# PEER block: U's two halves are summed on VectorE in place of TensorE, and semaphores stand in place of the drains in VectorE's chunk

## What is computed

```python
def chunk(args):
    ht, it, gt = args
    u = eu[it]
    a = jax.nn.gelu(jnp.einsum('ckd,cd->ck', u, ht).astype(jnp.float32), approximate=False) * gt
    return jnp.einsum('ck,ckd->cd', a.astype(ht.dtype), ev[it])
```

## Time and profile before

| | us |
|---|---|
| median of 3 runs | 1521.03 (1520.96 to 1522.51) |
| the profiled execution | 1529.37 |
| its span, first to last instruction | 1527.6 |
| PE busy in the span | 1489.6 (98%) |
| DVE busy | 1333.8 (87%) |
| POOL busy | 1028.9 (67%) |
| ACT busy | 760.4 (50%) |

### The profile page before, as it was taken

The page is one execution under the profiler, slowest core; times in us unless marked ns, Lnnn a source line. Parts: engine busy times, 40 slices in busy tenths (PEclk is TensorE's granted clock), DMA queues, the critical chain, the costliest instruction groups (busy, mean ns, idle before and its releaser), DMA issues.

```text
span 1527.6 us, 21852 instructions
## 1 busy us (share of the span) xinstructions
PE 1489.6 (98%) x7296; PEld 1236.3 (81%) x7296; DVE 1333.8 (87%) x2237; ACT 760.4 (50%) x1179; POOL 1028.9 (67%) x732
## 2 busy tenths in 40 slices
PE   7999999999999999999999999999999999999998
PEld 5887778888887888888878888888887888788886
DVE  6497666688998999989969999999999999999997
ACT  4644442433455555555455555454544555455553
POOL 6643224333886777778877777777777777777771
PEclk8999999899999999999999999999999999999999
DMA  9335447222776998989889999999999999999993
GB/s 361 98 104 173 154 149 266 79 83 83 220 237 191 284 293 278 293 278 315 285 299 396 396 389 401 370 377 393 393 388 360 380 398 395 368 390 395 396 404 129
DMA packets 219582, 444.58 MB, mean 291 GB/s; under 512 B 22360, under 2 KB 128984, under 8 KB 219232
## 3 DMA queue, kind: packets, MB, share of 16 engines
q1 hardware_dynamic: 174432, 309.04, 57.5%
q0 software_dynamic: 45056, 134.38, 23.1%
HBM read 407.68 MB, written 35.67 MB: 290 GB/s over the span
## 4 chain that ended last, share of the span: by engine, by line
PE 56%; POOL 27%; issue 8%; DMA 4%; DVE 3%; ACT 1%; DVEq 0%; SPq 0%; ACTq 0%; POOLq 0%
POOL coef L684 14%; POOL rows L678 13%; PE ps L1756 8%; PE ps L1757 8%; PE ps L1758 8%; PE ps L1505 4%; PE ps L1507 4%; PE ps L1506 4%; PE ps L1836 4%; PE ps L1805 2%; PE ps L1808 2%; PE ps L1811 2%; PE ps L1770 2%; PE ps L1838 2%; DMA coef<-gelu_spill,coef_at 2%
## 5 line engine op out<-in xcount | busy, mean ns | idle before, releaser
L635 POOL TENSOR_TENSOR wlo<-raw,whi 128x1024 fp32r<-128x1024 f32 x178 | 428.8, 2422 | 294.3 <-ACT whi L714 293.9
L1836 PE MATMUL ps<-acts,whi 128*128 128x512 f32 x1024 | 366.3, 397 | 0.0
L684 POOL DMA_INDIRECT coef<-gelu_spill,coef_at x256 | 299.5, 1170 | 82.0 <-issue 77.8
L678 POOL DMA_INDIRECT rows<-w_stream,row_at x256 | 273.0, 1067 | 78.0 <-issue 76.5
L1838 PE MATMUL ps<-acts,wlo 128*128 128x256 f32 x1024 | 287.3, 281 | 0.0
L714 ACT ACTIVATE whi<-raw 128x1024 fp32r<-128x1024 f32 x176 | 186.2, 1060 | 150.1 <-PE ps L1758 104.5
L1836 PEld LDWEIGHTS ps<-acts,whi 128*128 128x128 f32 x1024 | 192.7, 188 | 46.3
L1756 PE MATMUL ps<-whi,acts 128*128 128x512 f32 x512 | 200.7, 392 | 2.8 <-DVE gate_lo L1336 2.1
L1757 PE MATMUL ps<-wlo,acts 128*128 128x512 f32 x512 | 200.3, 391 | 0.0
L1758 PE MATMUL ps<-whi,acts 128*128 128x512 f32 x512 | 199.8, 390 | 0.0
L1838 PEld LDWEIGHTS ps<-acts,wlo 128*128 128x128 f32 x1024 | 193.6, 189 | 5.2
(11 more groups left out here) (253 smaller groups left out, 2582.8 us busy)
## 6 DMA issues: line engine op xcount, KB each, us to landing
raw<-w_stream SPq DMA_DIRECT2D x304, 512.0 KB, 5.4
values_in<-w_stream SPq DMA_DIRECT2D x128, 512.0 KB, 7.6
ada<-w_ada SPq DMA_DIRECT2D x32, 512.0 KB, 4.7
gelu_spill<-gout SPq DMA_DIRECT2D x64, 256.0 KB, 5.4
gate_spill<-gblock SPq DMA_DIRECT2D x8, 2048.0 KB, 10.4
gates<-gate_spill SPq DMA_DIRECT2D x32, 512.0 KB, 8.3
ada<-w_ada SPq DMA_DIRECT2D x32, 256.0 KB, 7.2
rows<-w_stream,row_at POOLq DMA_INDIRECT x256, 7.1
```

The source lines that it names most:

```text
L635: g.tensor_tensor(wlo[:, s, :], raw[:, s, :], whi[:, s, :].bitcast(F32), ALU.subtract)\
L678: g.indirect_dma_start(rows[m % ROWS][:, :], None, w_front.rearrange("c p n -> (c p) n"), bass.IndirectOffsetOnAxis(row_at[:, t * P + n:t ...
L684: g.indirect_dma_start(coef[:, t, n:n + 1], None, gelu_dram.rearrange("t p g (e o) -> (t p g e) o", o=1), bass.IndirectOffsetOnAxis(coef_a ...
L1836: mm(ps[:, 6 + e % PAIRED, :].rearrange("p (n t) -> p n t", n=2), wh, acts[:, :, k, 0:HALF], start=k == 0, stop=False)
```

## The change

`add_low` and its identity matrix go. VectorE gets `add_again(e)`, which adds `u_again(e, 0)` and `ulow` into a new SBUF tile `usum`; GELU reads `usum`. `again(e + 2)` on TensorE waits for that sum (it overwrites the bank) instead of for the GELU. The drains of the chunk go; `add_row(n, 0)` waits on semaphores instead, and `scale_coefs` is done at the end of the chunk before the one that needs it. GpSimd issues the coefficients of `n + 1` ahead of the rows of `n`.

```diff
@@ -221,8 +221,8 @@
         gelus = [gout[:, 2 * t:2 * t + 2, :].rearrange("p s n -> p (s n)") for t in range(PAIR)]
         prod = at("prod", 4, [P, RING, HALF], F32)
 
-        ulow = at("ulow", 24, [P, 2, HALF], F32R)
-        ident_r = at("ident_r", 26, [P, P], F32R)
+        usum = at("usum", 24, [P, 2, HALF], F32)
+        ulow = at("ulow", 26, [P, 2, HALF], F32)
         value_hi, value_lo = (w[:, PAIRED:2 * PAIRED, :] for w in (whi, wlo))
         phi = at("phi", 18, [P, PAIRED, HALF], F32R)
         plo = at("plo", 20, [P, PAIRED, HALF], F32R)
@@ -697,9 +697,9 @@
             for n in range(FIRST_COEFS):
                 fetch_coefs(n)
             for n in range(FIRST_ROWS, NK):
-                fetch_rows(n)
                 if n + FIRST_COEFS - FIRST_ROWS < NK:
                     fetch_coefs(n + FIRST_COEFS - FIRST_ROWS)
+                fetch_rows(n)
 
 
         @block.scalar
@@ -941,8 +941,6 @@
                 act.wait_ge(prod_ready, e + 1)
                 a.activation(phi[:, s % PAIRED, :], prod[:, s % PAIRED, :], ACT.Copy).then_inc(phi_ready, 1)
 
-            a.activation(ident_r[:, :], ident[:, :], ACT.Copy).then_inc(ident_ready, 1)
-
             def v_step(e, q, s, chunk=True, take=True):
 
                 act.wait_ge(chunk_used, e + (C_E + 1))
@@ -954,7 +952,7 @@
                     act.wait_ge(prod_ready, e - (RING - 1))
                 if PAIRED <= e < PAIRED + RING:
                     act.wait_ge(gelu_stored[s // 2], 16 * (NK // RING + 1))
-                a.activation(gelu_of(e), u_again(e, 0), ACT.Gelu).then_inc(gelu_done, 1)
+                a.activation(gelu_of(e), usum[:, e % 2, :], ACT.Gelu).then_inc(gelu_done, 1)
                 prod_hi(e, s)
                 if take:
                     value_take(e + 1, q + (s + 1) // RING, (s + 1) % RING)
@@ -1421,16 +1419,15 @@
             def scale_coefs(b):
                 dve.wait_ge(coef_in[b % COEF_RING], 16 * PAIR * COEFS * (b // COEF_RING + 1))
                 some = slice(b * COEFS, (b + 1) * COEFS)
-                v.tensor_tensor(coef[:, :, some], coef[:, :, some], gate_of[:, :, some], ALU.mult)
-                dve.drain()
+                v.tensor_tensor(coef[:, :, some], coef[:, :, some], gate_of[:, :, some], ALU.mult).then_inc(coefs_scaled, 1)
 
             def add_row(n, t):
 
+                m = n * PAIR + t
                 if t == 0:
-                    dve.drain()
-                    if n % COEFS == 0:
-                        scale_coefs(n // COEFS)
-                m = n * PAIR + t
+                    if n >= 1:
+                        dve.wait_ge(row_added, m)
+                    dve.wait_ge(coefs_scaled, n // COEFS + 1)
                 dve.wait_ge(row_in[m % ROWS], 16 * (m // ROWS + 1))
                 row, factor = rows[m % ROWS][:, :], coef[:, t, n:n + 1]
                 total = acc[:, t, :] if n == NK - 1 else sums[t]
@@ -1453,12 +1450,20 @@
                 v.tensor_tensor(plo[:, e % PAIRED, :], prod[:, e % PAIRED, :], phi[:, e % PAIRED, :].bitcast(F32),
                                 ALU.subtract).then_inc(plo_ready, 1)
 
+            def add_again(e):
+                dve.wait_ge(u_low_taken, e + 1)
+                v.tensor_tensor(usum[:, e % 2, :], u_again(e, 0), ulow[:, e % 2, :], ALU.add).then_inc(u_added, 1)
+
             make_value_lo(0)
             weights_normed(1)
             dve.drain()
             v.tensor_copy(gate_of[:, :, :].rearrange("p t n -> p (t n)"), fetched[2])
+            dve.drain()
             for e in range(NK):
                 due = [(n, t) for n in range(rows_done(e), rows_done(e + 1)) for t in range(PAIR)]
+                if e == BEHIND:
+                    scale_coefs(0)
+                add_again(e)
                 for n, t in due[:1]:
                     add_row(n, t)
                 make_prod(e)
@@ -1467,6 +1472,9 @@
                 prod_lo(e)
                 for n, t in due[1:]:
                     add_row(n, t)
+                for n in range(max(1, rows_done(e + 1)), rows_done(e + 2)):
+                    if n % COEFS == 0:
+                        scale_coefs(n // COEFS)
                 if e + 1 < NK:
                     make_value_lo(e + 1)
 
@@ -1811,22 +1819,18 @@
                     last = mm(dense_sums(t, half), plo[:, slot, column(t)], vh, start=False, stop=final, skip_group_check=True)
                 return last
 
-            def add_low(e):
-                pe.wait_ge(u_low_taken, e + 1)
-                mm(u_again(e, 0), ident_r[:, :], ulow[:, e % 2, :], start=False, stop=True,
-                   skip_group_check=True).then_inc(u_added, 1)
-
             def v_tile(e, s, final=False):
                 last = split_products(e, 1, final)
                 if final:
                     last.then_inc(dense_done, 1)
+                split_products(e, 0, final).then_inc(dense_done if final else values_used, 1)
+
+            def again(e, s):
+
+                if e >= PAIRED:
+                    pe.wait_ge(u_added, e - PAIRED + 1)
                 else:
-                    add_low(e + 1)
-                split_products(e, 0, final).then_inc(dense_done if final else values_used, 1)
-
-            def again(e, s):
-
-                pe.wait_ge(gelu_done, NK + 1 + e)
+                    pe.wait_ge(gelu_done, NK + 1 + e)
                 if not isinstance(e, int) or e >= POOL_LO:
                     pe.wait_ge(u_lo_ready, e - (POOL_LO - 1))
                 else:
@@ -1844,8 +1848,6 @@
                 mm(ps[:, b, 0:1], ident[:, :], zero[:, :], start=True, stop=True)
             for e in range(PAIRED):
                 again(e, e)
-            pe.wait_ge(ident_ready, 1)
-            add_low(0)
             for e in range(NK - PAIRED):
                 v_tile(e, e)
                 again(e + PAIRED, e)
@@ -1861,7 +1863,7 @@
                 turn(pair)
             v_tile(NK - 2, NK - 2)
             for n, pair in enumerate(TURNED_ORDER[2:]):
-                pe.wait_ge(gelu_done, 2 * NK + 1 + n)
+                pe.wait_ge(u_added, NK - 1 + n)
                 turn(pair)
             v_tile(NK - 1, NK - 1, final=True)
 
```

More of the change, by code:

```diff
@@ L365, in build @@
         u_low_taken = sem("u_low_taken")
-        ident_ready = sem("ident_ready")
         u_first_done = sem("u_first_done")
@@ L389, in build @@
         row_added = sem("row_added")
+        coefs_scaled = sem("coefs_scaled")
         turned = sem("turned")
@@ L1822, in v_tile @@
                     last.then_inc(dense_done, 1)
-                else:
-                    add_low(e + 1)
                 split_products(e, 0, final).then_inc(dense_done if final else values_used, 1)
             def again(e, s):
-                pe.wait_ge(gelu_done, NK + 1 + e)
+                if e >= PAIRED:
+                    pe.wait_ge(u_added, e - PAIRED + 1)
+                else:
+                    pe.wait_ge(gelu_done, NK + 1 + e)
                 if not isinstance(e, int) or e >= POOL_LO:
```

## The result

The changed kernel takes 1580.86 us (median of 4 runs, 1576.23 to 1583.62), the kernel before 1521.77 on the same chip: a ratio of 1.0373 [1.0333, 1.0413]. The forecast was 1525, with a range of 1516 to 1535. The direction was right, the size was not. The profiled execution took 1583.62 us, its span is 1581.8.

A forecast was written before the change was run, and what follows sets the result against it. It took VectorE's issue time plus its waits to be the V stage, with TensorE and GpSimd full too. Chunk work +9.3, waits -4.5 and the end -1 gave +3.8 us on 1521.0: 1525, range 1516 to 1535.

The forecast's parts named there:

- TensorE off the path: V stage: TensorE loses the identity product, 0.12 us a chunk, but VectorE needs more, so worth nothing by itself.
- The sum costs 0.33: VectorE's chunk: the added 256-column sum takes 0.33 us to the next start, at most 0.42.
- The rival with the sum not overlapped: VectorE's chunk: the sum costs 0.42 us in place of 0.33, +11 us, 1536; chance 0.13.
- the larger price for PSUM: VectorE's sum: by the skill's fixed cycles it would cost 0.065 us more, an estimated 8 us over the run.
- The drain and the scaling: VectorE's chunk: a drain less saves 0.17 us, and scaling falls from 0.24 to 0.07.
- parts 1 to 3 and 5: V stage: TensorE's relief nothing, VectorE's sum less drains and scaling +9.3 us, the end of the run -1 us.
- Four a chunk again: V stage: GpSimd still fits four fetches a chunk; VectorE's waits fall from 14.8 to 10.3 us, -4.5 us.
- Over 20 us of waits: Sign of a wrong forecast: VectorE's waits over 20 us; 6 to 14 us in all would be right.
- The end: Last chunks: the sum needn't wait behind TensorE's work, but VectorE, GELU and prod stand in a row: -1 us (0 to -2).
- GpSimd out of step: V stage: a fetch slips behind one more held instruction, 1.5 us; twelve slips are +18 us, 1540; chance 0.09.
- C: Theory of the experiments, V stage: the new fetch order makes rows late.

The follow-up runs named there:

- e9: Changed kernel without the second token group's coefficient fetches, so three fetches per pick: 1521.99 us, ratio 0.9993.
- e14: Kernel before without the second token group's coefficient fetches, three per pick: 1514.07 us, where the kernel before takes 1644.7.
- e7: Kernel before with only the fetch order swapped, coefficients ahead of rows: 1524.23 us, ratio 1.0011.
- e12: Kernel before with identity product kept on TensorE, no chunk drains, scaling a chunk ahead, coefficients fetched first: 1590.71 us, ratio 1.0426.
- e8: Changed kernel with one drain at the chunk's end, ahead of value_lo: 1549.03 us, ratio 1.0173.
- e11: Changed kernel with one drain ahead of each pick's first row: 1561.34 us, ratio 1.0252.
- e18: Changed kernel with one drain between plo and the second row: 1547.81 us, ratio 1.0157.
- e3: Kernel before with only the sum moved to VectorE, with old drains, scaling and order: 1577.97 us, ratio 0.9652, on a slow chip.
- e1: Changed kernel with one drain ahead of each pick's first row, on a slow chip: 1578.55 us, ratio 0.9659.
- e2: Changed kernel with rows fetched ahead of coefficients again, on a slow chip: 1614.9 us, ratio 0.988.
- e13: Changed kernel with the sum one chunk ahead, between the second row and value_lo, on a slow chip: 1643.71 us.
- e4: Kernel before without chunk drains, scaling a chunk ahead, coefficients fetched first, identity product kept on TensorE, on a slow chip: 1669.09 us, ratio 1.0224.
- e16: Changed kernel with the sum one chunk ahead, between the second row and value_lo: 1612.08 us, ratio 1.0555.

## Why the prediction was wrong, by its steps

1. TensorE off the path: right, and worth nothing. In the changed kernel it waits for `phi` (62.3 us in the waits above) and `plo`.
2. The sum costs 0.33: right, 817.66 to 817.99 in the timeline. The rival with the sum not overlapped did not occur. Neither did the larger price for PSUM of the Trainium skill (VectorE: DVE Perf Modes, the cycle table of the engines): by it, as an estimate, the sum would take 0.065 us more.
3. The drain and the scaling: right. The chunk above is 823.32 - 817.66 = 5.66 us, forecast 5.67. The two kernels with three fetches test the price of the change itself, with fetches out of the way: e9 takes 1521.99 us and e14, the kernel before with three, 1514.07, a difference of 7.9 us where parts 1 to 3 and 5 gave 9.3 - 1 = 8.3. They ran on different chips, so this is support and no proof.
4. **This step failed: "Fetches start at 0.05, 1.29 and 2.53; the last lies under `wlo`, ends at 3.90; ... Four a chunk again."** I let every held fetch through at the very next instruction, because 119 of 120 of before are. That is no law. Without the drain 50 of 118 miss it, the walk slips by 0.34 us, and the next fetch meets `value_lo` by a margin that I had not looked at. In my own walk it started at 4.20, with `value_lo` at 4.53: a slack of 0.33 us, and the slip is 0.34. The four fetches became 6.18 us, not 5.69, so GpSimd, put down as keeping step, is the bound by 6.18 - 5.705 = 0.475 us a chunk. In place of -4.5 us the waits gave +38 already between 800 and 1500 us: 21.5 + 20.0 + 11.7 = 53.2, where 14.8 stood. Over 20 us of waits was my own sign of being wrong.
5. The end: `value_lo` of the last chunk to the first `xt` takes 1568.80 - 1561.61 = 7.19 us, before 1515.02 - 1507.10 = 7.92. Forecast -1, measured -0.7:

```profile
1561.61 1.22 DVE L1445 TENSOR_TENSOR wlo<-values_in,whi 128x1024 fp32r<-128x1024 f32 x1
...
1568.80 3.22 DVE L1485 SCALAR_TENSOR_TENSOR xt<-ps,mod,xt 128x256 f32<-128x256 f32 x8
```

Two smaller faults. The fetch of 886.52, which I read as starting under an instruction with one SBUF input, starts 0.02 us ahead of the end of `value_lo` (885.32 + 1.22 = 886.54), which has two; it takes 0.94 us all the same. And twelve slips on top of 1525 are 1543, not 1540.

The right mechanism stood among the rivals, at 0.09: GpSimd out of step, by "a fetch that slips behind one more held instruction". Its price was a guess, twelve slips for 18 us, where the trace has 50 in the V stage, 28 of them with a second one.

What is shown, on the chips where the kernel before takes 1522 to 1524 us. The order of the fetches (C) costs nothing, by e7. GpSimd's four fetches are the bound of the changed kernel, by e9. Without the drains and with the scaling moved, and no other work added, the fetches grow to 1.254 us and the time by 67, by e12 beside e7. One drain in the chunk, at any of three places, gives back 18 to 33 us, by e8, e11 and e18.

What is not. No run has a pause of 0.17 us that is no drain, so whether the drain itself helps or the shift of 0.17 us in the pattern is open; e18, where 58 fetches still miss `plo` and only the next one is saved, speaks for the shift. No run parts the drains from the place of the scaling. The sum with the old drains (e3) was not run on such a chip. And why a fetch misses `plo` is open. In the changed kernel those that start 0.58 to 0.65 us into `wlo` miss it 50 times in 68, and all 27 that start 0.70 us or later pass. In e18 58 of the 60 at 0.64 to 0.66 us miss. But before, all 42 at 0.60 to 0.64 us pass, and in e8 all 112 at 0.59 to 0.65, with the same 1.13 or 1.14 us from `wlo` to `plo`.

What makes some chips slow is open too. It goes with the fourth fetch (e14 takes 1514 there), but not by the length of the fetches alone: e1 and e3 take 20 us more there than the sum gives for their mean fetch of 1.189 us, e2 31, e13 27 and e4 74. Between 800 and 1500 us GpSimd waits 31 to 50 us in e2, e4 and e13 for VectorE to use up rows. e1 and e11 are the same kernel on the two kinds of chip: their last fetches end at 1537.15 and 1537.45, and their spans (1575.4 and 1565.4) 38.2 and 28.0 us later, so there 10 us lie behind the fetches.

On the chips where the kernel before takes 1522 to 1524 us no version beat it with all its work. On the slow chip of e1 to e4 three did: e1 and e3 are 3.4% and 3.5% faster than the kernel before there, e2 1.2%. e14, with TensorE busy for all of 700 us, says what a lighter GpSimd could give where the kernel before takes 1522: at best 1514, 0.5%, an estimate across two chips.

## What to carry to other kernels

When an engine's busy share reads 67%, add the gaps between its instructions before calling it free: GpSimd's are 150 us of 700 and none of them is usable. Where two engines share a resource in a fixed pattern, work out the slack of every meeting point, and price what happens when the closest one is missed by one instruction. A drain that looks like 0.17 us of waste can be what keeps two engines in step; take it away alone first, and look at the other engine's mean duration. And when one engine's instructions can hold another's, a longer mean duration does not say which of the two is the bound: count what each needs for a chunk.

## What the hardware showed beyond expectation

- An indirect fetch on GpSimd takes 0.94 us when free. Held by a VectorE instruction with two SBUF inputs, it ends 0.90 us after the start of the VectorE instruction at which it is let through, and that need not be the next one. The Trainium skill (SBUF — State Buffer, Who interferes with whom) says, of VectorE's modes that use two ports for one tensor, that whoever issues first has the shared ports for the whole instruction. The traces agree for one instruction with two SBUF inputs, and show besides that a fetch already waiting can lose the boundary to VectorE's next: up to 2.71 us in e4 and e16, past two boundaries.
- Nearly every missed boundary has a 256-column instruction on one side of it (`prod` to `wlo`, `wlo` to `plo`, `plo` to `wlo`, `value_lo` to `prod`). Between the second row and `value_lo`, both of 1024 columns, fetches went through, 118 of 121 at `value_lo`'s start before. Whether the length is the reason was not tried.
- The same kernel takes 1522 us on some chips and 1638 to 1645 on others, a difference of 8% that is gone with three fetches per pick (1514 on a slow chip).
